# Attention of two layers with twelve blocks made four: transposes, running sums and rope moved beside other stages

## The reference, cut to what matters

```python
def _layer(x, positions, g_mix, w_in, b_forget, w_branch, w_out, g_mlp, w_up, w_down):
    h = _rmsnorm(x, g_mix)
    proj = h @ w_in
    (qa, ka, va, qb, kb, vb, fl, qc, kc, vc, qi, ki, wi, gl) = jnp.split(proj, COL_SPLITS, axis=-1)
    br_a = _stick_breaking_attention(heads(qa, SB_HEADS), heads(ka, SB_HEADS), heads(va, SB_HEADS))
    log_f = jax.nn.log_sigmoid((fl + b_forget).astype(jnp.float32))
    br_b = _forgetting_attention(heads(qb, FOX_HEADS), heads(kb, FOX_HEADS),
                                 heads(vb, FOX_HEADS), log_f)
    qc = _partial_rope(heads(qc, DSA_HEADS), positions).reshape(b, s, DSA_KV_HEADS, DSA_GROUP, HEAD_DIM)
    ...
    br_c = _indexed_sparse_attention(qc, kc, vc, qi, ki, wi, top_k)
    gates = jax.nn.sigmoid(gl.reshape(b, s, N_BRANCH, D_MODEL))
    y = (gates[:, :, 0, :] * (br_a @ w_branch[0])
         + gates[:, :, 1, :] * (br_b @ w_branch[1])
         + gates[:, :, 2, :] * (br_c @ w_branch[2]))
    x = x + y @ w_out
    ...
```

## Time and profile before

| | before |
|---|---|
| time, median of 3 runs | 2722.35 us (2721.1 to 2722.99) |
| the profiled execution's own time | 2726.9 us |
| its span | 2725.1 us |
| PE busy | 2556.0 us (94%) |
| DVE busy | 1705.4 us (63%) |
| ACT busy | 1362.3 us (50%) |
| mean granted clock of PE | 0.962 |

### The profile page before, as it was taken

How to read it: one execution, slowest core, us unless ns; L and a number is a source line. 1 busy time by engine, 2 the same in 40 slices (tenths; PEclk the granted TensorE clock), 3 DMA queues, 4 the chain that set the end, 5 groups by cost and what they waited for, 6 DMA issues and landing times. The chain is left out here.

```text
span 2725.1 us, 34406 instructions
## 1 busy us (share of the span) xinstructions
PE 2556.0 (94%) x13721; PEld 2095.2 (77%) x13721; DVE 1705.4 (63%) x1943; ACT 1362.3 (50%) x1520; POOL 105.8 (4%) x154
## 2 busy tenths in 40 slices
PE   6999999999999999998799897999999999999996
PEld 6774479987754799878699886878787888888785
DVE  3434355544343555656644546788888888888887
ACT  4421244444312444533344344677777777777775
POOL 0100010001000100014000000000000000000000
PEclk9988999999889999989899897999999999999998
DMA  9141255541412555520555503999999999999996
GB/s 331 67 155 62 101 185 186 186 162 67 155 62 95 186 185 186 119 75 1 186 173 168 192 1 124 363 363 358 341 356 360 359 343 363 355 357 343 361 360 216
DMA packets 391567, 586.58 MB, mean 215 GB/s; under 512 B 21168, under 2 KB 284656, under 8 KB 391280
## 3 DMA queue, kind: packets, MB, share of 16 engines
q1 hardware_dynamic: 391408, 584.37, 63.1%
HBM read 580.13 MB, written 4.19 MB: 214 GB/s over the span
## 5 line engine op out<-in xcount | busy, mean ns | idle before, releaser
L3107 DVE TENSOR_TENSOR moe_low<-ring,moe_high 128x2048 fp32r<-128x2048 f32 x288 | 658.3, 2290 | 109.1 <-ACT moe_high L3071 103.9
L3071 ACT CAST moe_high<-ring 128x2048 fp32r<-128x2048 f32 x288 | 549.2, 1907 | 171.6 <-PE bank L3008 90.1
L3002 PE MATMUL bank<-moe_high,moe_xh 128*128 128x512 f32 x896 | 240.6, 390 | 7.9 <-PEq L2827 7.9
L3002 PE MATMUL bank<-moe_low,moe_xh 128*128 128x512 f32 x896 | 240.6, 390 | 0.0
L3002 PE MATMUL bank<-moe_high,moe_xl 128*128 128x512 f32 x896 | 240.3, 390 | 0.0
L3002 PEld LDWEIGHTS bank<-moe_high,moe_xh 128*128 128x128 f32 x896 | 168.6, 188 | 43.2 <-issue 8.1
L3002 PEld LDWEIGHTS bank<-moe_high,moe_xl 128*128 128x128 f32 x896 | 168.7, 188 | 35.2
L3002 PEld LDWEIGHTS bank<-moe_low,moe_xh 128*128 128x128 f32 x896 | 168.7, 188 | 35.2
L3008 PE MATMUL bank<-moe_high,moe_hh 128*128 128x512 f32 x448 | 128.8, 409 | 15.4 <-DVE moe_hl L3112 8.1
L1784 DVE TENSOR_TENSOR chain_low<-upper_ring,chain_high 128x2048 fp32r<-128x2048 f32 x36 | 82.5, 2292 | 95.4 <-ACT chain_high L1757 95.4
L1757 ACT CAST chain_high<-upper_ring 128x2048 fp32r<-128x2048 f32 x36 | 68.5, 1904 | 117.1 <-PE bank L1729 58.6
(11 more groups left out here) (503 smaller groups left out, 4814.9 us busy)
## 6 DMA issues: line engine op xcount, KB each, us to landing
ring<-in_moe_w_gate SPq DMA_DIRECT2D x206, 512.0 KB, 5.1
ring<-in_moe_w_up SPq DMA_DIRECT2D x206, 512.0 KB, 7.0
ring<-in_moe_w_down SPq DMA_DIRECT2D x88, 1024.0 KB, 7.4
ring<-in_w_in SPq DMA_DIRECT2D x18, 2048.0 KB, 8.3
xT<-in_moe_w_down SPq DMA_DIRECT2D x25, 1024.0 KB, 7.4
upper_ring<-in_w_in SPq DMA_DIRECT2D x10, 2048.0 KB, 8.1
upper_ring<-in_w_up SPq DMA_DIRECT2D x10, 2048.0 KB, 8.1
...
```

The costliest lines, as they stand in the source:

```text
L3002: mm = pe.matmul(core.banks[i % 2][:], (xl if other_low else xh)[:, place(m), 4 * part + c, :], wt[:, c, :], start=(part == 0 and j == 0 a ...
L3071: act.copy(unit(high, u), ring.raw(u)).then_inc(s["weight_high"], 1)
L3107: dve.tensor_tensor(unit(low, u), ring.raw(u), unit(high, u), ALU.subtract)\
```

## The change

The chain of twelve blocks becomes four: stick, bc_proj, forget with index, sparse with gate.

- `FirstTurn` is the `side` of bc_proj. At unit 0 PE makes the 8 transposes of the first branch (banks 4 and 5), at unit 1 ACT and DVE copy them. At units 17 to 19 DVE and ACT make what `decay_stage` made, at unit 20 PE makes the three small products, at unit 21 DVE copies the sums.
- `softmax_stage` becomes `softmax_part`, which returns lists instead of a block; the window attention of the second block runs it alone, as before. In "forget" DVE turns one rope group after heads 1, 3, 5 and 7.
- `index_part` follows "forget" in the same block, on every engine behind it. It holds b_turn, the layout of rope, c_fold, the indexer, and two gate tiles; PE makes the 32 gate products in pieces (5, 3, 3, 5, 16) between the other steps, the second tile in banks 4 and 5.
- `gate_part` follows "sparse" in the same block. PE starts on the first branch at once, and c_turn comes after half of the second.
- Nothing is computed otherwise. `br`, `cum` and `tmp` lie in the lower arena now. The semaphores of gate logits are one; a semaphore less is used in `gdn_out_stage`.

The core of the diff, leading blanks of moved lines not counted as a difference:

```diff
-def softmax_stage(core, tag, at, heads, q, k, v, mask, out, bias=None, sink=None, ready=None, logits=None,
-                  beside=None):
...
+def softmax_part(core, tag, at, heads, q, k, v, mask, out, bias=None, sink=None, ready=None, logits=None, beside=None,
+                 rope=None):
...
                     dve.tensor_scalar(minus[:, h, :], top[:, h, :], -1.0, None, ALU.mult).then_inc(s["negated"], 1)
+            if rope is not None and i % 2 and i // 2 < rope.GROUPS:
+                rope.turn(dve, i // 2)
...
+                                  total[:, hs, t:t + 1].broadcast_to([P, per_bank, HD]), ALU.mult).then_inc(s["out"], 1)
...
-def decay_stage(core, tag, fl, b, cT, tmp):
+class FirstTurn:
...
+    def pe(self, pe, u):
+        core, s = self.core, self.s
+        if u == 0:
+            for n in range(2):
+                turn_chunks(core, pe, core.banks[4 + n], self.rows, range(2 * n, 2 * n + 2)).then_inc(s["turned"], 1)
+        if u == 20:
+            pe.wait_ge(s["step"], 4)
+            bank = core.banks[6]
+            pe.matmul(bank[0:8, 0:P], self.u2[:, 0, :], core.const("le"), start=True, stop=True)
+            pe.matmul(bank[0:8, P:T], self.u2[:, 0, :], core.const("ones"), start=True, stop=False)
+            pe.matmul(bank[0:8, P:T], self.u2[:, 1, :], core.const("le"), start=False, stop=True).then_inc(s["sums"], 1)
...
+    def act(self, act, u, act_stored, dve_stored):
+        s, e = self.s, self.e
+        if u == 1:
+            act.wait_ge(s["turned"], 1)
+            keep_turned(self.core, act, self.turned, self.core.banks[4], range(0, 2))
+        if u == 18:
+            act.wait_ge(s["step"], 2)
+            act.activation(e, e, ACT.Exp).then_inc(s["log"], 1)
+            act.wait_ge(s["log"], 1)
+            act.activation(e, e, ACT.Ln, bias=1.0).then_inc(s["log"], 1)
...
+    def dve(self, dve, u, act_stored, dve_stored):
+        core, s, e = self.core, self.s, self.e
+        if u == 1:
+            dve.wait_ge(s["turned"], 2)
+            keep_turned(core, dve, self.turned, core.banks[5], range(2, 4))
+        if u == 17:
             dve.wait_ge(core.bias_there, 16 * DEPTH)
+            dve.wait_ge(act_stored, 4)
+            dve.wait_ge(dve_stored, 4)
             for t in range(NT):
...
+                op = dve.tensor_tensor(self.u2[:, t, :], self.fl[:, t, :], self.b, ALU.add)
...
+        if u == 19:
             dve.wait_ge(s["step"], 3)
...
+            dve.wait_ge(s["log"], 2)
+            dve.tensor_tensor(self.u, self.u, e, ALU.add).then_inc(s["step"], 1)
+        if u == 21:
             dve.wait_ge(s["sums"], 1)
...
-def rope_stage(core, tag, proj, flat, cos, sin, tmp, logits):
+class Rope:
...
+    def turn(self, dve, group):
+        s, half = self.s, ROT // 2
+        (a, b), t = ((8, ROPE_COLS[0]), ROPE_COLS[1:3])[group // NT], group % NT
...
+        if group:
+            dve.wait_ge(s["rotated"], group)
                     dve.tensor_tensor(u[0], x1, c, ALU.mult)
                     dve.tensor_tensor(u[1], x2, si, ALU.mult)
                     dve.tensor_tensor(u[2], x2, c, ALU.mult)
                     dve.tensor_tensor(u[3], x1, si, ALU.mult).then_inc(s["parts"], 1)
-                    done += 1
-                    dve.wait_ge(s["parts"], done)
+        dve.wait_ge(s["parts"], group + 1)
                     dve.tensor_tensor(x1, u[0], u[1], ALU.subtract)
                     dve.tensor_tensor(x2, u[2], u[3], ALU.add).then_inc(s["rotated"], 1)
...
+    def lay_queries(self, act):
+        act.wait_ge(self.s["rotated"], self.GROUPS)
             for t in range(NT):
-                act.mul(flat[:, t, 0:512], proj[:, t, 8:520], HD ** -0.5)
-                act.copy(flat[:, t, 768:1024], proj[:, t, 776:1032])
+            act.mul(self.flat[:, t, 0:512], self.proj[:, t, 8:520], HD ** -0.5).then_inc(self.s["queries"], 1)
+            act.copy(self.flat[:, t, 768:1024], self.proj[:, t, 776:1032]).then_inc(self.s["queries"], 1)
...
+    def lay_keys(self, pool):
+        pool.wait_ge(self.s["rotated"], self.GROUPS)
             for t in range(NT):
...
-def indexer_stage(core, tag, at, cT, wi, mask, logits):
+def index_part(core, tag, at, forget, earlier, rope, rows, turned, cT, wi, mask, first, second):
...
+    fold_banks = [core.banks[b] for b in (2, 3, 4, 5, 0)]
+    fold_chunks = [range(2 * n, min(2 * n + 2, 9)) for n in range(5)]
...
+    def pe_program(pe):
+        pe.wait_ge(earlier.stored, earlier.kept)
+        first.some(pe, 0, 5)
+        pe.wait_ge(forget["out"], NT)
+        for n in range(2):
+            turn_chunks(core, pe, core.banks[n], rows, range(2 * n, 2 * n + 2)).then_inc(s["turned"], 1)
+        first.some(pe, 5, 8)
+        pe.wait_ge(rope.s["queries"], rope.LAID)
+        pe.wait_ge(rope.s["keys"], NT)
+        for n in range(5):
+            if n == 4:
+                pe.wait_ge(s["kept"], 2)
+            turn_chunks(core, pe, fold_banks[n], rope.flat, fold_chunks[n]).then_inc(s["folded"], 1)
+        first.some(pe, 8, 11)
+        pe.wait_ge(s["kept"], 2)
+        pe.wait_ge(s["act_folded"], 3)
+        pe.wait_ge(s["dve_folded"], 2)
             for h in range(HI):
                 r = slice(HD * (h % 2), HD * (h % 2) + HD)
                 for t, (a, b) in enumerate(edges):
                     mm = pe.matmul(core.banks[h][:, a:b], cT[r, 6 + h // 2, t * P:(t + 1) * P], cT[r, 8, 0:b - a],
                                    start=True, stop=True)
                 mm.then_inc(s["dots"], 1)
-            logits.all(pe)
+        first.some(pe, 11, 16)
+        second.some(pe, 0, 16)
...
+    def act_program(act):
+        act.wait_ge(forget["summed"], HEADS)
+        rope.lay_queries(act)
+        act.wait_ge(s["turned"], 1)
+        keep_turned(core, act, turned, core.banks[0], range(0, 2)).then_inc(s["kept"], 1)
+        for n in (0, 2, 4):
+            act.wait_ge(s["folded"], n + 1)
+            keep_turned(core, act, cT, fold_banks[n], fold_chunks[n]).then_inc(s["act_folded"], 1)
...
+    def dve_program(dve):
+        dve.wait_ge(s["turned"], 2)
+        keep_turned(core, dve, turned, core.banks[1], range(2, 4)).then_inc(s["kept"], 1)
+        for n in (1, 3):
+            dve.wait_ge(s["folded"], n + 1)
+            keep_turned(core, dve, cT, fold_banks[n], fold_chunks[n]).then_inc(s["dve_folded"], 1)
...
+def gate_part(core, tag, at, w, first, branches, logits, y, sparse, earlier, rows):
-def gate_stage(core, tag, at, w, first, branches, logits, y):
...
+        w.wait(pe, first)
+        for half in range(2):
+            products(0, half)
+        w.wait(pe, first + 1)
+        pe.wait_ge(sparse["out"], NT)
+        products(1, 0)
+        pe.wait_ge(s["product"], 2)
+        for n in range(2):
+            turn_chunks(core, pe, core.banks[n], rows, range(2 * n, 2 * n + 2)).then_inc(s["turned"], 1)
+        pe.wait_ge(earlier.stored, earlier.kept)
+        products(1, 1)
+        w.wait(pe, first + 2)
+        pe.wait_ge(s["kept"], 2)
+        for half in range(2):
+            products(2, half)
...
             for b in range(NB):
+            if b == NB - 1:
+                act.wait_ge(s["turned"], 1)
+                keep_turned(core, act, branches[b], core.banks[0], range(0, 2)).then_inc(s["kept"], 1)
+                act.wait_ge(earlier.stored, earlier.kept)
                 for n in range(4):
                     act.activation(logits[b][:, n, :], logits[b][:, n, :], ACT.Sigmoid).then_inc(s["sigmoid"], 1)
...
             for b in range(NB):
+            if b == 1:
+                dve.wait_ge(s["turned"], 2)
+                keep_turned(core, dve, branches[NB - 1], core.banks[1], range(2, 4)).then_inc(s["kept"], 1)
                 for n in range(4):
...
-    decay_stage(core, "decay", core.cproj[:, :, 0:8], core.b_forget[:, i, :], cum, tmp)
-    softmax_stage(core, "forget", end, 8, head_rows(qT), head_rows(kT), lambda h, j: v[:, j, h * HD:(h + 1) * HD],
...
-    turn_stage(core, "b_turn", br, brT[1], BW // P)
...
-    rope_stage(core, "rope", core.cproj, flat, core.cos, core.sin, tmp,
-               GateLogits(core, "rope", w, base + 12, logits[1], (1,)))
-    third_at = end
-    cT, end = core.part(end, 9, T)
-    turn_stage(core, "c_fold", flat, cT, 9)
...
+    forget, of_forget = softmax_part(
+        core, "forget", free, 8, head_rows(qT), head_rows(kT), lambda h, j: v[:, j, h * HD:(h + 1) * HD],
+        lambda h, t: core.const("neg")[:, P * t:P + 2 * P * t], br,
+        bias=(lambda h: core.const("ident")[0:8, h:h + 1].broadcast_to([8, P]), cum[0:8, :]), logits=gates[0], rope=rope)
...
-    indexer_stage(core, "index", scratch, cT, core.cproj[:, :, 1096:1100], mask,
...
+    run_both(core, forget, index_part(core, "index", scratch, of_forget, gates[0], rope, br, brT[1], cT,
+                                      core.cproj[:, :, 1096:1100], mask, gates[1], gates[2]))
...
-    turn_stage(core, "c_turn", br, brT[2], BW // P)
-    gate_stage(core, "gate", end, w, base + 15, brT, logits, core.flat_xT())
```

(6 more changed lines are left out.)

610 lines of the change are left out of this document (268 added, 342 removed).

## The result

The changed kernel took 2694.16 us, median of 4 runs (2684.61 to 2701.21), against 2722.67 us before (4 runs, 2721.10 to 2726.18): a ratio of 0.9891 [0.9852, 0.9931]. Faster, as forecast, but outside the range: the gain is 28 us, not 52. The profiled execution took 2687.89 us, span 2685.8; it lies under its median and that of before over its own, so the two traces stand 39 us apart and the medians 28. In six more runs (the first experiment) the median was 2691.13. A run over 1.5% above the fastest of its kernel, at a lower granted clock, is left out of the ratios as slow; three runs of the spread kernel are the only ones.

The account below looks back on a forecast made before the run. PE, busy 94% of the span, was taken as the path, losing time in holes between blocks and at the lower clock. Terms of 2.5 + 4.0 + 6.6 + 8.25 + 4.7 = 26.05 us a layer, 52.1 for two, gave 2670 us, within 2662 to 2677.

Parts of the forecast that it names:

- Parts 1 and 2: First branch's transposes beside bc_proj save 2.5 us a layer; decay block moved into bc_proj saves 4.0 us a layer.
- Part 4: Second branch's transposes, rope, fold and indexer joined behind "forget" without holes on PE: 8.25 us a layer, bounds 4.8 and 8.3.
- rule to weigh: Transposes between gate products act like a hole for the clock: two falls a layer, 2677 us; added nothing to a chance.
- Part 5: Gate products start directly behind "sparse", third branch's transposes among them: 4.7 us a layer, bounds 3.0 and 4.9.
- Part 3: "forget" starts at the full clock, so 13.2 us of work at 0.50 halves: 6.6 us a layer, bounds 3.2 and 10.2.
- gate products between all scores: Argument against the rival that the clock falls inside the joined blocks: two falls more per layer, 2677 us, chance 0.2.
- the slower rival: "forget", gate products and transposes stay at clock 0.50 through the whole joined block: up to 2818 us, chance 0.02.
- 'forget' doesn't keep its early clock at all: Worse case of the clock falling inside the joined blocks: 13.2 us lost, 2683 us; chance 0.2 for that rival as a whole.

Follow-up runs that it names:

- the first experiment: The changed kernel run again with nothing altered: 2691.13 us, median of 6 runs, ratio 0.9879.
- the spread kernel: Changed kernel with the 16 gate products of "forget" spread evenly, one between a head's score blocks and one behind: 2711.83 us, ratio 0.9853 of three runs.
- 128 rows: Sums' products given 128 rows (120 of zeros) instead of 8: on the old kernel 2716.17 us; on the changed kernel 2674.90 us, again 2670.89 us.
- the products first: Changed kernel with 128-row sums and each head's gate products ahead of its scores in "forget" and "sparse": 2665.82 us, again 2666.45 us.
- 128-row kernel: Changed kernel with the sums' products at 128 rows, 120 of them zeros, instead of 8: 2674.90 us, again 2670.89 us.
- 8 rows and wide products ahead: Changed kernel, 8-row sums: each head's gate products ahead of its scores, 2673.40 us; all 16 of "forget" ahead of its first head, 2709.41 us.
- the kernel without the sums: Changed kernel with the 8-row products of the running sums left out of the scores of "forget": 2654.26 us, ratio 0.9735.
- the one spread: Changed kernel with 128-row sums and gate products spread evenly, one between a head's score blocks and one behind, in "forget" and "sparse": 2679.54 us.

## Why the prediction was wrong

**Parts 1 and 2 were right.** 6.54 and 6.85 us a layer against 6.5. The 8 transposes start at 108.29 behind the first barrier, and bc_proj's first wide product at 110.31 behind a wait of 0.96; the forecast had about 110.5 and 1.0. The earlier trace rows had it at 112.54. The decay products stand before the 76-column products, and "forget" follows after one barrier of 0.93.

**Part 4 was right**, in structure and size: 34.35 us in both layers, forecast 34.5. Of the waits on PE only the one for the previous logits shows, 0.32 us at 219.94, as the forecast had it; the layouts and folds had their cover, and DVE's mask was done at 248.3, before PE's last gate product. The transposes were no hole: the earlier trace rows had it so, and the stretch at 1.00 above confirms it. This trace does not show the falls that the prediction drew from its rule to weigh (the Trainium skill, "TensorE: Matmul & The Clock Gate", Part 4: PE-mode transpose): 8 and 18 transposes, 1.04 and 2.13 us of them, stand between groups of three to five gate products, and the clock stays at 1.00.

**Part 5 was right**: 5.09 and 5.05 us against 4.7, directly behind the last head.

**Part 3 is the step that failed**: "'forget' starts warm", 6.6 us in each layer with bounds 3.2 and 10.2. It was 4.8 in layer 0 and -4.7 in layer 1, and "sparse" in layer 1 lost 3.2 more. Together that is 13.2 - 0.1 + 3.2 = 16.3 us short; the other parts gave 1.4 more than asked, and 2.1 came from elsewhere: 52.1 - 16.3 + 1.4 + 2.1 = 39.3, the distance of the two traces. The medians lie 28.5 apart. The other 10.5 us are that before's profiled run lay 4.2 over its median and after's 6.3 under; they are put down to the clock by the runs' mean granted clocks alone (0.969 at 2684.61, 0.960 at 2701.21), as no run near 2700 has a trace. Two sentences carried it. The first took it that two pieces "with the clock at 0.50 throughout" would take half: that assumed the hole ahead was the only cause of their low clock. It is one of two: with 128 rows the hole alone still gives 6.5 and 10.5 us of it, and with 8 rows "forget" is low behind a mere barrier of 0.9 us. (That hole began at 175.81, not at 176.1, which changes nothing here.) The second was the "against" of the rival, "gate products between all scores", taken as keeping the clock up; the spread kernel shows that gate products can stand between all scores and the clock stay at 0.50 for 47.7 us. The reason against the slower rival, "the clock rose at 194.66 in the middle of 'forget'", was no bound either: in after it rose only after 27 us. That rival ("once low, the narrow products don't raise it") came nearest to the mechanism that the runs show, at a chance of 0.02 and for the whole block; it acts in "forget" alone and ends there. The rival "'forget' doesn't keep its early clock at all", 2683 by price, was the nearest case to the 2691 to 2694 measured.

The lower bound of part 3 should have been nothing, and the rows held that. The falls at 205 and 212 us without a hole said that in this block a fall needs no cause outside. What a fall can cost there is then not 1.7 us but half the length of a low stretch, and the long ones in "forget" were 13.2 and 13.6 us: half of one is the whole 6.6 us of part 3. That the part could go below nothing, with a stretch of 27.3 us, no row of before showed.

**The sum.** With 128 rows the change gains 39 to 41 us, and 128 rows by themselves gain 10. With the products first the whole is 60 us below before (2726.14 - 2666.45). So the forecast's 52 us were there to be had, but not by this change alone.

**What stays open.** Why one execution of the same list falls and another does not: the changed kernel ran 2684.61 to 2701.21, at granted clocks of 0.969 to 0.960; and in one execution the stretch ends in layer 0 ahead of the third head and in layer 1 ahead of the fifth. What brings the clock down is less shown than what keeps it down. The fall at 696.9 in layer 1 has only 0.6 us of narrow products behind the barrier, a 128-row kernel fell at 693.5 too, and with 8 rows and wide products ahead it still fell at 181.7 and at 196.3. Only the kernel without the sums (one trace), the 128-row kernel with the products first (two) and the one spread (one) kept 1.00 through "forget" in each trace. What the chip counts when it lowers the clock is not measured here. Between 8 and 128 rows no kernel was run, so whether 64 would do is untried. Why the start of "sparse" still falls in some executions and not in others, with the products behind or spread, no run separates. Which of the spread kernel's heads were low in its runs of 2723 us and more is not known.
